# Sliding-window heads of a two-layer encoder: wide score matmuls, a new order of the weight units, and the last head pair beside the output projection

## What is computed

```python
h = x @ w_in                                  # columns: A value/gate, B q/k/v/gate, C q/k/v/gate
b_q, b_k = rope_partial(b_q), rope_partial(b_k)        # rotary on the first 16 of 64 dims
s = (q . k) * 64**-0.5                        # B: 16 heads, 2 key/value heads, window: own + previous chunk of 64
p = softmax(concat([s, sink]))[..., :-1]      # one sink logit per head
b_out = (p @ v) * silu(b_gate)
a_out, c_out = ...                            # pooling mixer; attention over 9 chunks with a bias
y = concat([a_out, b_out, c_out]) @ w_out
x = layer_norm(2**0.5 * x + y)
```

## Time and profile before

| | |
|---|---|
| median of 3 runs | 2903.08 us (2900.37 to 2904.02) |
| the profiled execution | 2902.22 us |
| its span, first to last instruction | 2900.4 us |
| granted TensorE clock | 0.999 of full speed |
| busy: PE, PE weight loads, DVE, ACT, POOL | 99%, 83%, 55%, 44%, 44% |

### The profile page before, as it was taken

One profiled execution on the slowest core, in us unless ns is written; L12 is line 12 of the kernel. 1 busy time (PEld: TensorE's weight loads), 2 busy tenths in 40 slices (PEclk: granted clock), 3 DMA queues, 4 the chain that ended last, 5 costly groups with the idle time before them and its releaser, 6 DMA issues.

```text
span 2900.4 us, 46215 instructions
## 1 busy us (share of the span) xinstructions
PE 2866.1 (99%) x13776; PEld 2399.6 (83%) x13776; DVE 1601.1 (55%) x2834; ACT 1278.1 (44%) x2683; POOL 1261.8 (44%) x926
## 2 busy tenths in 40 slices
PE   8999999999999999999999999999999999999998
PEld 6888888888888888888888888888888888888886
DVE  5555666522667766651156666664126667666424
ACT  5444455422444445542244444654224444455421
POOL 4444444444444434444444444444444444444441
PEclk9999999999999999999999999999999999999999
DMA  6434323454444432345454443234554444233442
GB/s 195 123 121 121 87 84 85 130 171 157 135 146 142 141 84 77 90 120 156 150 168 146 149 146 90 77 85 141 165 154 140 129 142 141 84 84 83 127 156 102
DMA packets 189148, 364.14 MB, mean 126 GB/s; under 512 B 18912, under 2 KB 27136, under 8 KB 185344
## 3 DMA queue, kind: packets, MB, share of 16 engines
q1 hardware_dynamic: 185264, 347.25, 39.7%
q10 hardware_dynamic: 3792, 15.73, 1.4%
HBM read 320.94 MB, written 45.11 MB: 126 GB/s over the span
## 4 chain that ended last, share of the span: by engine, by line
PE 93%; DVE 4%; issue 3%; ACT 1%; POOL 0%; DVEq 0%; ACTq 0%; POOLq 0%
PE acc L540 64%; PE sc L540 18%; PE pv L540 8%; PE sc L601 2%; PE sc L639 1%; DVE prob L1356 0%; DVE nmax L1347 0%; DVE mx L1346 0%; ACT mixh L873 0%; DVE nmax L1315 0%; DVE sc L1313 0%; PE acc L570 0%; PE pv L564 0%; PE sc L564 0%; DVE brope L1356 0%
## 5 line engine op out<-in xcount | busy, mean ns | idle before, releaser
L1225 POOL TENSOR_TENSOR wl<-raw,wh 128x512 fp32r<-128x512 f32 x920 | 1261.1, 1375 | 1595.0 <-ACT wh L873 1568.4
L540 PE MATMUL acc<-xh,wh 128*128 128x512 f32 x2624 | 1036.6, 395 | 12.7 <-DVE xl L1257 8.5
L540 PE MATMUL acc<-xh,wl 128*128 128x512 f32 x2624 | 1024.1, 390 | 0.0
L540 PE MATMUL acc<-xl,wh 128*128 128x512 f32 x2624 | 1023.7, 390 | 0.0
L873 ACT ACTIVATE wh<-raw 128x512 fp32r<-128x512 f32 x920 | 571.6, 631 | 982.5 <-PE acc L540 669.2
L540 PEld LDWEIGHTS acc<-xh,wh 128*128 128x128 f32 x2624 | 493.7, 188 | 114.7 <-issue 12.4
L540 PEld LDWEIGHTS acc<-xh,wl 128*128 128x128 f32 x2624 | 493.2, 188 | 105.6
L540 PEld LDWEIGHTS acc<-xl,wh 128*128 128x128 f32 x2624 | 494.1, 188 | 94.7
L540 PE MATMUL sc<-wh,mixh 128*128 128x512 f32 x496 | 193.4, 390 | 0.1
L540 PE MATMUL sc<-wh,mixl 128*128 128x512 f32 x496 | 193.1, 389 | 0.0
L540 PE MATMUL sc<-wl,mixh 128*128 128x512 f32 x496 | 192.9, 389 | 0.0
(11 more groups left out here) (201 smaller groups left out, 3629.9 us busy)
## 6 DMA issues: line engine op xcount, KB each, us to landing
raw<-in_wall SPq DMA_DIRECT2D x920, 256.0 KB, 2.7
res_scratch<-res ACTq DMA_DIRECT2D x12, 1024.0 KB, 4.5
res<-res_scratch SPq DMA_DIRECT2D x12, 1024.0 KB, 4.9
res<-in_x SPq DMA_DIRECT2D x8, 1024.0 KB, 5.3
x_scratch<-res SPq DMA_DIRECT2D x8, 1024.0 KB, 4.7
prob<-x_scratch SPq DMA_DIRECT2D x32, 256.0 KB, 3.4
res<-x_scratch SPq DMA_DIRECT2D x8, 1024.0 KB, 5.3
hist_scratch<-mixh SPq DMA_DIRECT2D x8, 768.0 KB, 4.4
```

Source lines behind the costliest of these rows:

```text
L540: return nc.tensor.matmul(o, lhsT, rhs, start=start, stop=stop)
L1225: nc.gpsimd.tensor_tensor(wl[:, s, :], raw[:, s, :], wh[:, s, :].bitcast(F32), ALU.subtract).then_inc(w_lo, 1)
```

## The change

- The keys and their remainders lie side by side (`b_keys`), and `b_scores` makes one matmul of 2 x 128 columns for a chunk; its parts stand next to each other in `sc[g]` (chunks 0 to 3) and `pv` (4 to 7). `b_max` first adds the parts with a `tensor_reduce` of 4 x 128 x 2 elements into `prob` or, for odd pairs, into the new `odd_scores`, takes the maximum there, and `b_exp` works in place there.
- The iteration becomes eight units for each head pair; the first four units are the gate tile, the eight behind them the two query tiles. The transposes come in two groups of four. The first iteration stands outside the loop.
- The second query tile is projected before the values.
- `rope_copy` goes: `rotate` reads PSUM.
- The scores, transposes and attend of the last pair are put between row tiles of output units 1, 5, 6 and 8. `X_AT`, `X_LOAD` and the `res` loads move back, half of the x transposes go to even banks. Both output loops are written out.
- In the last step the wait for the last gate moves from ahead of the output projection to the fourth row tile.

```diff
-X_AT = (2, 3, 5, 7, 9, 11, 13, 14)
-X_LOAD = (6, 6, 9, 11, 13, 15, 17, 19)
+X_AT = (11, 12, 13, 14, 20, 22, 24, 26)
+X_LOAD = (14, 15, 18, 19, 24, 26, 28, 30)
...
-                        if s in (14, 30):
+                        if s in (18, 30):
...
             def b_scores(it, v, g):
-                    mm(o, q, bk[g][:, ks], True, False)
-                    last = mm(o, q, bkl[g][:, ks], False, True)
+                    last = mm(b_parts[g][c // 4][:, c % 4, :, unseen:P], q, b_keys[g][:, :, ks], True, True)
...
                     quarter(0)
-                    quarter(1)
                     b_scores(it, t * 2, 0)
-                    quarter(2)
-                    b_scores(it, t * 2 + 1, 1)
-                    quarter(3)
+                    for s in range(1, 4):
+                        quarter(s)
                     pe.wait_ge(gate_ok, t * 2 + (MIXES * it + 2 * C_PAIRS + 1))
                     quarter(4)
-                    quarter(5)
-                    b_transpose(it, t * 2, 0)
+                    b_transpose(it, t * 2, 0, 0)
+                    quarter(5, range(0, 2))
+                    b_transpose(it, t * 2, 0, 1)
+                    quarter(5, range(2, 4))
                     quarter(6)
-                    quarter(7)
+                    quarter(7, range(0, 2))
                     b_attend(it, t * 2, 0)
+                    quarter(7, range(2, 4))
+                    quarter(8)
+                    b_scores(it, t * 2 + 1, 1)
...              (units 9 to 15 as 1 to 7, with the odd pair)
+                def last_tile(k, t):
+                    v = B_TILES - 1
+                    if (k, t) == (1, 3):
+                        b_scores(it, v, 1)
+                    if (k, t) in ((5, 3), (6, 1)):
+                        b_transpose(it, v, 1, 0 if k == 5 else 1)
+                    if (k, t) == (8, 1):
+                        b_attend(it, v, 1)
...
             def b_max(it, v, g):
+                    V_(V.tensor_reduce(probs(v, g)[:, u, :, :], b_parts[g][u].rearrange("p c l k -> p c k l"), AX, ALU.add))
-                    V_(V.tensor_reduce(mx[:, n, :], b_sc[g][:, u, :, :], AX, ALU.max, negate=True))
+                    V_(V.tensor_reduce(mx[:, n, :], probs(v, g)[:, u, :, :], AX, ALU.max, negate=True))
...
             def rotate(it, n, r, bank, scale=SCALE):
-                V.tensor_tensor(y_, x_, brope[:, 0, :], ALU.mult)
-                V_(V.stream_shuffle(x_, x_, SWAP))
-                V_(V.tensor_tensor(x_, x_, brope[:, 1, :], ALU.mult))
+                V.scalar_tensor_tensor(y_, acc[bank][:, :], scale, brope[:, 0, :], ALU.mult, ALU.mult)
+                V.stream_shuffle(x_, acc[bank][:, :], SWAP).then_inc(rope_raw, 1)
+                V_(V.scalar_tensor_tensor(x_, x_, scale, brope[:, 1, :], ALU.mult, ALU.mult))
                 V.tensor_tensor(x_, x_, y_, ALU.add).then_inc(rope_ok, 1)
...
+                    if not first:                      # VectorE, one iteration
+                        b_product(it, i - 2, 0)
                     sinks_of(it, i)
                     b_max(it, i, 0)
+                        mix_lo_of(i - 2)
+                        b_product(it, i - 1, 1)
+                    b_normalise(it, i, 0, (0,))
+                        mix_lo_of(i - 1)
+                    b_normalise(it, i, 0, (1,))
+                    gate_of(i, 0)
+                    b_lo(it, i, 0)
+                    b_add(it, i, 0, (0,))
+                    rotate(it, i + 3, i * U_B + (B0 + U_B + 7), 1)
                     b_max(it, i + 1, 1)
                     rotated_query(i + (ROTS * it + 4), 0)
+                    b_add(it, i, 0, (1,))
                     b_normalise(it, i + 1, 1)
+                    rotate(it, i + 4, i * U_B + (B0 + U_B + 11), 0)
                     b_lo(it, i + 1, 1)
                     rotated_query(i + (ROTS * it + 5), 1)
                     b_add(it, i + 1, 1)
-                    b_product(it, i, 0)
-                    mix_lo_of(i)
                     gate_of(i + 1, 1)
-                    b_product(it, i + 1, 1)
```

More of the change, by code:

```diff
@@ L290, in build @@
         bs_full = sem("bs_full")
+        b_read = sem("b_read")
         bs_max = sem("bs_max")
@@ L473, in _ @@
                 for s in range(U_B):
-                    load_unit(it, B0 + s, s % RING)
+                    load_unit(it, B0 + s, s % RING, B0 + (s + 4) % U_B)
                 with sp.Fori(0, TWOS - 1) as t:
-                    for s, first in enumerate((12, 20, 8, 16)):
+                    for s, first in enumerate((8, 12, 20, 16)):
                         for q in range(4):
@@ L732, in _ @@
[L732 to L738, removed]
+                    project(it, B0 + s, s, acc[0][:, :], s % RING)
+                for s in range(4):
+                    project(it, B0 + 4 + s, s, v_bank, s % RING)
@@ new lines, in two_tiles, with gate_unit @@
+                    b_transpose(it, t * 2 + 1, 1, 1)
+                    quarter(13, range(2, 4))
+                    quarter(14)
+                    quarter(15, range(0, 2))
+                    b_attend(it, t * 2 + 1, 1)
+                    quarter(15, range(2, 4))
+                two_tiles(0, True)
+                with pe.Fori(1, TWOS - 1) as t:
+                    two_tiles(t, False)
+                def gate_unit(s, part=range(4)):
+                    project(it, O0 - U_B + s, s % 4, acc[s // 4][:, :], s % RING, part)
@@ L788, in _ @@
                     break
-                with pe.Fori(0, 2) as m:
+                for m in range(2):
                     for n in range(2):
@@ L957, in b_exp, with b_hi @@
                 act.wait_ge(bs_max, v * 2 + (2 * B_TILES * it + u + 1))
-                if not (isinstance(v, int) and v == B_TILES - 1):
-                    act.wait_ge(bt_full, v * 2 + 2 * B_TILES * it)
-                else:
-                    act.wait_ge(rope_ok, (B_TILES + 1) * (it + 1))
                 nc.scalar.activation(esink[:, n, :], nmax[:, n, :], ACT.Exp, bias=sink1[:, g, 0:1])
                 for c in range(4):
-                    last = nc.scalar.activation(probs(v)[:, u, c, :], b_sc[g][:, u, c, :], ACT.Exp, bias=nmax[:, n, c:c + 1],
+                    last = nc.scalar.activation(probs(v, g)[:, u, c, :], probs(v, g)[:, u, c, :], ACT.Exp,
+                                                bias=nmax[:, n, c:c + 1],
                                                 accum_out=psums[:, n, c:c + 1])
                 last.then_inc(bs_exp, 1)
-            def b_hi(it, v, g):
-                for u in range(2):
+            def b_hi(it, v, g, fours=range(2)):
+                for u in fours:
                     act.wait_ge(bt_full, v * 2 + (2 * B_TILES * it + u + 1))
@@ L1190, in _ @@
                                 x_hi(it + 1, m, gg)
-                        split(it, m * (2 * U_N) + (O0 + 2 + s), (s + 2) % RING)
+                        if m == 0 and s < U_N:
+                            out_slot(s + 2)
+                        else:
+                            split(it, m * (2 * U_N) + (O0 + 2 + s), (s + 2) % RING)
                         if s % U_N == U_N - 1:
@@ L1573, in two_tiles @@
                     rotated_query(i + (ROTS * it + 5), 1)
-                    b_lo(it, i + 1, 1)
-                    gate_of(i, 0)
                     b_add(it, i + 1, 1)
-                    b_product(it, i, 0)
-                    mix_lo_of(i)
                     gate_of(i + 1, 1)
-                    b_product(it, i + 1, 1)
                 section(total)
-                two_tiles(0, False)
+                two_tiles(0, True)
+                total += count[1]
                 with dv.Fori(1, TWOS - 1) as t:
-                    section(t * per_t + total)
-                    two_tiles(t * 2, True)
+                    section(t * per_t + (total - per_t))
+                    two_tiles(t * 2, False)
```

364 lines of the change are left out of this document (195 added, 169 removed).

## The result

| | before | after |
|---|---|---|
| median of the runs beside each other | 2903.1 us (2900.4 to 2904.0) | 2944.6 us (2940.7 to 2945.5) |
| ratio, 95% interval | | 1.0143 [1.0131, 1.0155] |
| span of the profiled execution | 2900.4 us | 2943.4 us |
| granted TensorE clock | 0.999 | 0.994 |

Forecast were 2875 us and a chance of 0.09 for slower. The change costs 41 us.

What follows compares the result with a forecast made beforehand. PE, busy 99% of the span, was taken as the bound. Terms: -26.9 scores, +0.3 split, +0.3 returns to projection, -9.6 waits, +7.2 lateness = -28.7 us; 2903.1 becomes 2874.4, say 2875, range 2864 to 2893 (chance 0.8).

Steps and rivals of the forecast that it cites:

- Scores, -26.9 us: Score matmuls on PE: a wide block takes 0.95 us instead of 1.79, saving 0.84 us for each of 32 pairs.
- Addition 1.22 us: DVE's new additions of 1024 elements, four an iteration, take 1.22 us each, bounds 1.1 and 1.8.
- the slower rival: DVE sets the pace: gain gone at an addition of 1.8 us, 2922 us at 2.1; chance 0.09.
- Rotation from PSUM at nothing for PE: Rotation reading PSUM takes a copy of about 0.6 us from ACT, none on PE's path; cosine product 0.69 us.
- Waits removed, -9.6 us: PE's gaps before a step's first scores, the last pair but one's attend and the last output projection go: 9.6 us.
- x transposes and loads at nothing: Moved x and `res` loads and x transposes hold nothing up; without the cover 1 to 2 us each, 8 us.
- Split transposes, 0.3 us: Two groups of four transposes cost PE 32 x 0.01 = 0.3 us, 1.7 at most.
- Expected lateness: DVE late at the even transposes by 0.6 us, 12 times, 7.2 us in all, bounds 0 and 20; odd ones nothing.
- DVE "not the bound by its load": DVE has 38.6 us of work in an iteration of 49.5 us, so order matters, not load.
- The rival "costs more than it gives back in part": DVE's queue: additions of 1.4 to 1.6 us or more hits; 2883 to 2897 us; chance 0.18.

Runs made afterwards that it cites:

- e5: On top of e2: odd pair's second fold and the first product behind the even maxima, rotation's second half behind the odd maxima, normalises together; 2869.6 us.
- e6: e5 with narrow scores: two matmuls of 128 columns a chunk added in PSUM, no addition on DVE; 2896.9 us.
- e9: e7 with the rotation again by way of a ScalarE copy instead of reading PSUM; 2871.9 us, ratio 0.9887.
- e3: The changed kernel with narrow scores: two matmuls of 128 columns a chunk added in PSUM, no addition on DVE; 2896.9 us.
- e7: e5 with the eight transposes of a pair in one group again, where the second group of four stood; 2867.0 us.
- e11: e7 with each addition of the score parts done twice; 2902.6 us, ratio 0.9990.
- e10: The changed kernel, order untouched, with POOL making the weights' remainder for 256 of 512 columns only; 2878.2 us.
- e8: The changed kernel with e2's new order of the even pair alone, the odd pair's queue as in the change; 2912.4 us.
- e1: The changed kernel with the odd pair's first normalise ahead of the query's remainder and the second fold behind both; 2913.0 us.
- e2: e1 plus the even pair: one product and both `mix_lo` behind the normalise each had preceded, ScalarE's `mix_hi` likewise; 2884.6 us.

## Why the prediction was wrong

- **Scores, -26.9 us: right.** 0.95 us a block; 27.3 us by e5 against e6.
- **Addition 1.22 us: right**, and with it the break-even of the slower rival (1.8 us) was not reached. The sign of that rival came true by another way.
- **Rotation from PSUM at nothing for PE: not contradicted** (e9, in the late order). The cosine product took 0.69.
- **Waits removed, -9.6 us: right** for those named; e3 shows 6.7 us net of small new ones. The last pair's scores brought 1.8 us that had no term.
- **x transposes and loads at nothing, at most 8 us:** 1.4 us.
- **Split transposes, 0.3 us with 1.7 as the bound:** 2.5 us by the medians, not told apart from either.
- **"Expected lateness: 0.2 to 0.9 us, I take 0.6. The odd transposes have about 0.7 us of slack after the same count and I give them nothing": this step failed.** 7.2 us were forecast with 20 as the bound, 59.2 came. The count of instructions was nearly right, their lengths were not. It took three or four meetings of 0.7 us as a mean in the even run and gave the odd run none. The 0.7 was read from a product that started 0.44 us into a POOL instruction of 1.29; one that starts earlier loses more. The trace has four of 0.9 to 1.1 us in the even run, 4.0 us, against 1.9 us of room: 2.1 us late, where PE waits 2.4 in all. It has four of 1.0 to 1.1 us in the odd run, 4.2 us, against 0.7 us of room: 3.5 us late, and 3.6 is what PE shows in each of the later iterations of first-half steps. A bound "all hits, and the odd transposes too" should have counted every instruction with two inputs in SBUF, the minimum of four numbers and the folds included, at the rest of a POOL instruction (up to 1.3 to 1.5 us); it stopped at 1.7 us for each iteration.
- **The places are fixed, not drawn by lot.** The mean of `prob`'s product is 1164 ns and that of `odd_scores` 692 ns, both of one kind: of the first 16 in 32 take 1580 to 1800 ns, at the same places in each step, and the rest 691 to 694; of the second none of 24 is met. Second-half steps, without the `MEMSET` of 0.11 us, have 1.39 us of wait at the odd transposes where the others have 3.64: the minimum and the fold there miss POOL. In e7 the first odd product of each pair is met (1.60 us) and the second never (0.69), a mean of 1148 ns.
- **The clock had no term.** 13.0 us came from TensorE at 1.2 GHz behind waits that the forecast held for absent. Behind one wait of 3.4 to 3.6 us the matmuls lost 1.4 to 2.9 us more.
- **DVE "not the bound by its load": right in effect, wrong in number.** 38.6 us were forecast, 44.5 measured. The 5.9 between are meetings, to within 0.6: the iteration after has eight, 8.1 us in all, and the one before had two, 1.6 us, which its 33.7 already held. e7 hides 43.4 us in 49.3; with 4.9 more in e11 the runs no longer fit.
- **The rival "costs more than it gives back in part", 2883 to 2897:** its own terms do not give this range; 12 x 0.9 to 16 x 1.6 on 2868 are 2879 to 2894.

The cause is settled: e5 takes the loss away by order alone, e10 by shorter POOL instructions alone, e3 by leaving out the additions. What stays open is why the stretches at half speed have the length they have, and why one long wait in twelve has none.

## What to carry to other kernels

Where an engine feeds the bound one through a chain without a break, sum the whole run to each due time with every instruction that can meet another engine at its worst, and compare the room with that, for each chain and not for the one that looks tightest. Work on which nothing waits soon (remainders, folds, products of earlier pairs) belongs behind what the bound engine waits for: here the same instructions in another order are worth 75 us, and turn a loss of 1.4% into a gain of 1.1 to 1.2%.

## What the runs showed of the hardware that was not expected

- In the B stage of the changed kernel a DVE instruction with two operands in SBUF that starts while POOL runs, or as it starts, ends 0.0 to 0.6 us after POOL does, however small it is: 1.35 us for four numbers a partition that take 0.23 otherwise. The end comes 0.02 us behind POOL's for four elements a partition, 0.28 for 256 and 0.55 for 512, so the loss is the rest of POOL's instruction less 0.1 to 0.2 us (1.14 left: 0.69 becomes 1.69; 0.67 left: 1.22; 0.29 left: 0.83). One already under way was not lengthened. Additions from PSUM (1.21 to 1.23 us) and maxima in SBUF (0.69) never took longer. The Trainium skill, "SBUF - State Buffer", section Who interferes with whom, says that an instruction with two SBUF inputs contends with GpSimd and a `tensor_reduce` on trn2 never does; the trace agrees, and adds how long one meeting lasts.
- Behind a wait of PE of 3.4 to 3.6 us the granted clock fell to 0.50 in eleven of the twelve cases of the two kernels that have them (the changed kernel and e8), for 3.4 us or, in three cases, 6.8. Behind waits of 1.4 to 2.0 us alone it did not (the second-half steps, e1, e2). In e11 it did three times behind waits of 0.6 and 1.6 to 1.7 us whose starts are 1.1 us apart, and twice it did not behind the same pair.
- Where DVE's queue lacks a `MEMSET` of 0.11 us (second-half steps), PE's wait at the odd transposes is 2.2 us shorter, since two meetings of about 1 us each, of the minimum and of the fold, are absent there. That the 0.11 us alone decided both is not shown by a run of its own.
